# A two-block transformer step on one core: memory values computed in the expert loop, gate and up as two products, norms applied after the products

## The reference, cut to what matters

```python
def first_block(...):
    ...
        h = h + mixed @ w_out[l]
        h = h + hier_moe(rms_norm(h, norm2_gain[l]), w_group[l], b_group[l], w_expert[l],
                         b_expert[l], w_gate[l], w_up[l], w_down[l])
    return rms_norm(h, final_gain)

# one expert: w_gate, w_up 1024 x 512, w_down 512 x 1024
        h = jax.nn.silu(xb @ w_gate[e]) * (xb @ w_up[e])
        return h @ w_down[e]

def second_block(...):
        h = rms_norm_2(x, g_pre_mix[l])
        proj = h @ w_in[l]
        ...
        mem_n = rms_norm_2(mem, g_mem[l])
        c = cross_attention(h, mem_n, w_cq[l], w_ckv[l], w_co[l])

def cross_attention(h, mem_n, w_cq, w_ckv, w_co):
    kv = mem_n @ w_ckv
    k = split_heads(kv[..., :D_MODEL], CROSS_HEADS)
    v = split_heads(kv[..., D_MODEL:], CROSS_HEADS)
```

## Time and profile before

| | us |
|---|---|
| median of three runs | 1629.61 (1627.13 to 1630.34) |
| the profiled execution | 1629.03 |
| its span in the trace | 1627.2 |
| the loop's first expert product | 200.1 |
| last expert's down product | 1120.7 |
| first `in2` product | 1158.9 |

### The profile page before, as it was taken

The page is one execution under the profiler, slowest core; times in us unless marked ns, Lnnn a source line. Parts: engine busy times, 40 slices in busy tenths (PEclk is TensorE's granted clock), DMA queues, the critical chain, the costliest instruction groups (busy, mean ns, idle before and its releaser), DMA issues.

```text
span 1627.2 us, 21987 instructions
## 1 busy us (share of the span) xinstructions
PE 1215.0 (75%) x9589; PEld 752.2 (46%) x9589; DVE 318.9 (20%) x677; ACT 251.4 (15%) x582; POOL 49.3 (3%) x82
## 2 busy tenths in 40 slices
PE   7999956655655665565665565567999899999997
PEld 4566733323432332333332333333445385888843
DVE  1532312211211211221221121122024213100001
ACT  3321311111110110111111111011021212100000
POOL 4101000000000000000000000001000000000000
PEclk9999988978888987997997898898999999999999
DMA  9314499999999999999999999999633251444320
GB/s 351 142 53 163 155 404 430 426 430 427 430 427 430 427 430 427 431 427 431 427 431 427 431 427 431 427 430 403 246 106 104 75 173 51 159 150 147 134 81 28
DMA packets 83105, 493.15 MB, mean 303 GB/s; under 512 B 4768, under 2 KB 28528, under 8 KB 58496
## 3 DMA queue, kind: packets, MB, share of 16 engines
q1 hardware_dynamic: 81088, 486.69, 73.3%
q0 software_dynamic: 1600, 5.17, 1.0%
q10 hardware_dynamic: 384, 0.82, 0.1%
HBM read 491.61 MB, written 1.05 MB: 303 GB/s over the span
## 4 chain that ended last, share of the span: by engine, by line
PE 47%; DMA 46%; DVE 3%; issue 1%; ACT 1%; POOL 1%; SPq 1%; POOLq 0%; DVEq 0%; ACTq 0%
DMA ring<-in_w_up_dram 45%; PE bank L909 10%; PE bank L1141 9%; PE bank L548 6%; PE bank L999 5%; PE bank L1172 5%; PE bank L627 3%; PE bank L568 1%; PE bank L647 1%; DMA ring<-in_w_in_dram 1%; PE bank L536 1%; SPq L381 1%; POOL stat L472 1%; PE bank L764 0%; PE bank L744 0%
## 5 line engine op out<-in xcount | busy, mean ns | idle before, releaser
L909 PE MATMUL bank<-ring,big 128*32 128x256 f32 x4096 | 305.7, 464 | 252.1 <-DMA ring<-in_w_up_dram 234.8
L909 PEld LDWEIGHTS bank<-ring,big 128*32 128x32 f32 x4096 | 174.1, 133 | 378.9 <-issue 342.4
L923 PE MATMUL bank<-ring,big 128*32 128x256 f32 x2048 | 123.8, 382 | 75.5 <-DVE big L1795 62.1
L1141 PE MATMUL bank<-xT,ring 128*128 128x256 f32 (+1 forms) x832 | 153.3, 347 | 0.8 <-issue 0.8
L1141 PEld LDWEIGHTS bank<-xT,ring 128*128 128x128 f32 x832 | 138.0, 191 | 16.5 <-issue 1.6
L1790 DVE TENSOR_TENSOR big<-big,bank 128x128 f32<-128x128 f32 x64 | 23.7, 371 | 525.3 <-ACT big L1355 525.3
L923 PEld LDWEIGHTS bank<-ring,big 128*32 128x32 f32 x2048 | 63.4, 109 | 135.9 <-DVE big L1795 78.9
L1355 ACT ACTIVATE big<-bank 128x128 f32<-128x128 f32 x64 | 17.8, 278 | 511.8 <-PE bank L909 511.8
L548 PE MATMUL bank<-ring,xT 128*128 128x512 f32 x192 | 86.7, 610 | 3.0 <-DVE xT L1478 3.0
L999 PE MATMUL bank<-ring,xT 128*128 128x512 f32 x192 | 86.2, 602 | 0.6 <-ACT xT L1208 0.6
L1799 DVE COPY big<-bank 32x256 f32<-32x256 f32 x128 | 54.3, 424 | 134.7 <-PE bank L923 133.9
(11 more groups left out here) (268 smaller groups left out, 871.0 us busy)
## 6 DMA issues: line engine op xcount, KB each, us to landing
ring<-in_w_gate_dram SPq DMA_DIRECT2D x64, 2048.0 KB, 18.3
ring<-in_w_up_dram SPq DMA_DIRECT2D x64, 2048.0 KB, 22.7
ring<-in_w_down_dram SPq DMA_DIRECT2D x64, 2048.0 KB, 25.1
ring<-in_w_gate_up_dram SPq DMA_DIRECT2D x22, 1024.0 KB, 7.2
ring<-in_w_in_dram SPq DMA_DIRECT2D x14, 1024.0 KB, 12.1
ring<-in_w_down_dram SPq DMA_DIRECT2D x8, 1024.0 KB, 6.5
ring<-in_w_in_dram SPq DMA_DIRECT2D x3, 2048.0 KB, 22.9
ring<-in_w_ckv_dram SPq DMA_DIRECT2D x2, 2048.0 KB, 12.9
```

The lines of the kernel that those rows point to most:

```text
L909: i = pe.matmul(bank[q % 2][TOK * j:TOK * (j + 1), 0:SEQ], xg[:, k, TOK * q:TOK * (q + 1)], w[:, :, k, j * P:(j + 1) * P], start=(k == 0), ...
L923: i = pe.matmul(bank[6 + q % 2][TOK * m:TOK * (m + 1), 0:SEQ], hT[:, q % 2, TOK * k:TOK * (k + 1)], w[:, k, SEQ * m:SEQ * (m + 1)], start= ...
L1141: i = pe.matmul(bank[j % 4][:, gu * SEQ + lo:gu * SEQ + hi], w[:, k, gu, (j % 2) * P:(j % 2 + 1) * P], xT[:, k, lo:hi], start=(k == 0), st ...
```

## The change

- **Memory values in the loop.** The value half of `w_ckv_2` (4 MiB) is no longer part of the weights after the loop. SP loads it before the loop, half into `aux` behind the second expert unit, the rest into `xT` and `mix` once the router has read them. In each pass, between gate and up of q = 3, PE computes 64 of its 1024 columns for both tiles (`memory_values`, 16 products of 64 columns); ACT copies them out, and POOL moves the result to `c_v` after the loop.
- **Gate and up** are two products of 128 columns (32 products each); gate goes to banks 0 and 1, up to bank 5, and each slot is freed by its own product (`moe_g`, `moe_gu`).
- **The pass.** The gather no longer waits for `sel_gate`; its transposes come behind the gather. Combining goes tile by tile.
- **Deferred norms.** After the loop PE transposes the raw `x` tile by tile, the gains of both norms are one product in `col_gain`, and the two rstd factors (`in2_scale`) are applied when `in2` is evacuated. The constants of the second block (`c2`) are loaded from `moe_x` on, as the memory rows stand there until then.
- **Before the loop.** The router works on tables of 8 experts per token, the number of rounds is found before the gates, the mix of tile 0 is finished earlier, and filler steps are moved: 10 and 10 around the transposes of the mix (8 and 8 before), 8 ahead of the loop (12 before). The first gain and three POOL loads move at the start.
- **After the loop** the next norm's transposes stand behind the third product step of the last product (`third`), the out transposes of tile 0 no longer wait for the silu of tile 1, and one evacuation and one maximum are exchanged.

```diff
-                sp.wait_ge(*at("moe_d" if part == "down" else "moe_gu", n))
+                sp.wait_ge(*at({"gate": "moe_g", "up": "moe_gu", "down": "moe_d"}[part], n))
...
+                rows = chunks(t_in["w_ckv_2"][0])[:, :, D:2 * D]
+                if u == 1:
+                    sp.dma_start(aux[:, 0:4 * D].rearrange("p (k c) -> p k c", k=4), rows[:, 0:4, :]).then_inc(S("cvw_in"), 16)
+                if u == 4:
+                    sp.wait_ge(*at("route_mm", TT))
+                    sp.wait_ge(*at("n2_n", TT))
+                    sp.dma_start(xT_[:, :].rearrange("p (k c) -> p k c", k=2), rows[:, 4:6, :]).then_inc(S("cvw_in"), 16)
+                    sp.dma_start(mix_[:, :].rearrange("p (k c) -> p k c", k=2), rows[:, 6:8, :]).then_inc(S("cvw_in"), 16)
...
+            pool.wait_ge(*at("moe_x", 1))
+            load(c2[:, 0:consts["c2"].shape[1]], consts["c2"], "c2_in")
             load(row_gain[:, 0, :], t_in["g_post_mix_2"][0:1, :].to_broadcast([P, D]), "postmix_in")
             for t in range(TT):
                 rstd_tile("pm", t, 38)
+                pool.wait_ge(*at("pm_rstd", t + 1))
+                pool.tensor_tensor(in2_scale[:, t:t + 1], stat[:, 38 + t:39 + t], stat[:, 6 + t:7 + t], ALU.mult
+                                   ).then_inc(S("in2_scale"), 1)
+            for t in range(TT):
+                pool.tensor_copy(c_v[:, t, :], moe_v[t]).then_inc(S("cv_ev"), 1)
...
-            keys(8)
-            wait_T("mix", 0)
+            transposes("mix", mix, 0, 2)
+            keys(10)
             pe.wait_ge(*at("mix_n", 2))
             transposes("mix", mix, 1, 4)
-            keys(8)
+            keys(10)
+            wait_T("mix", 0)
...
-            keys(12)
-            pe.wait_ge(*at("ck_ev", 4))
+            keys(8)
...
-                def hidden_pair(q):
-
-                    arrive("gate", q)
-                    arrive("up", q)
...
+                def hidden(part, q, dst, signal):
+
+                    arrive(part, q)
+                    w = slot(PRE_UNITS + MOE_UNITS.index((part, q))).rearrange("p (k c) -> p k c", k=KD)
                     for k in range(KD):
                         for j in range(4):
-                            i = pe.matmul(bank[q % 2][TOK * j:TOK * (j + 1), 0:SEQ], xg[:, k, TOK * q:TOK * (q + 1)],
-                                          w[:, :, k, j * P:(j + 1) * P], start=(k == 0), stop=(k == KD - 1),
+                            i = pe.matmul(dst[TOK * j:TOK * (j + 1), 0:P], xg[:, k, TOK * q:TOK * (q + 1)],
+                                          w[:, k, j * P:(j + 1) * P], start=(k == 0), stop=(k == KD - 1),
                                           tile_position=(0, TOK * j))
-                    i.then_inc(S("moe_gu"), 1)
+                    i.then_inc(S(signal), 1)
+
+                def memory_values():
+
+                    pe.wait_ge(*at("cvw_in", 48))
+                    pe.wait_ge(*at("moe_v_ev", it + 1))
+                    for t in range(TT):
+                        for k in range(KD):
+                            i = pe.matmul(bank[4][:, t * CV_COLS:(t + 1) * CV_COLS], memT[:, k, t * P:(t + 1) * P],
+                                          cv_weights[k][:, bass.ds(b * CV_COLS, CV_COLS)], start=(k == 0), stop=(k == KD - 1))
+                    i.then_inc(S("moe_v"), 1)
...
                         i.then_inc(S("moe_xg_mm"), 1)
+                pe.wait_ge(*at("moe_selg", it + 1))
+                for t in range(TT):
+                    i = pe.transpose(bank[5][:, t * P:(t + 1) * P], sel_gate[:, t, :], ident)
+                i.then_inc(S("moe_selT_tp"), 1)
                 pe.wait_ge(*at("moe_xg_a", it + 1))
                 pe.wait_ge(*at("moe_xg_v", it + 1))
+                pe.wait_ge(*at("moe_selT", it + 1))
                 for q in range(BATCH):
-                    hidden_pair(q)
+                    hidden("gate", q, bank[q % 2], "moe_g")
+                    if q == BATCH - 1:
+                        memory_values()
+                    hidden("up", q, bank[5], "moe_gu")
                     down(q)
 
...
+                for n in range(4):
+                    t, half = n // 2, n % 2
+                    if n >= 2:
...
-            pe.wait_ge(*at("moe_x", 1))
-            for u in range(2):
-                post_linear("cv", "mm", memT, u, u)
-
-            for t in range(TT):
-                transposes("pm", xn, t)
-            emptied("cv", 2)
+            for t in range(TT):
+                pe.wait_ge(S("moe_xadd"), rounds * (4 * NB) + 1 + 2 * t)
+                transposes("pm", x, t, 4 + 2 * t)
...
-                    act.wait_ge(*at("moe_gu", it * BATCH + q + 1))
+                    act.wait_ge(*at("moe_g", it * BATCH + q + 1))
                     A(eg[:, q % 2, :], bank[q % 2][:, 0:P], ACT.Silu).then_inc(S("moe_e"), 1)
+                    if q == BATCH - 1:
+                        act.wait_ge(*at("moe_v", it + 1))
+                        for t in range(TT):
+                            i = A(moe_v[t][:, bass.ds(b * CV_COLS, CV_COLS)], bank[4][:, t * CV_COLS:(t + 1) * CV_COLS], ACT.Copy)
+                        i.then_inc(S("moe_v_ev"), 1)
...
-            squares("fin", x, 6, mix, lambda t: act.wait_ge(*at("moe_x", 1)))
+            for t in range(TT):
+                act.wait_ge(S("moe_xadd"), rounds * (4 * NB) + 1 + 2 * t)
+                square("fin", x, 6, mix, t)
+                evac_T("pm", 1, tiles=(t,))
...
             def in2_evac(u):
                 act.wait_ge(*at("in2_mm", 2 * u + 1))
-                A(proj2[:, 0, IN2_UNITS[u]:IN2_UNITS[u] + 512], bank[0][:, :], ACT.Copy).then_inc(S("in2_ev0"), 1)
+                if u == 0:
+                    act.wait_ge(*at("in2_scale", 1))
+                if u == 4:
+                    act.wait_ge(*at("cv_ev", TT))
+                A(proj2[:, 0, IN2_UNITS[u]:IN2_UNITS[u] + 512], bank[0][:, :], ACT.Copy, scale=in2_scale[:, 0:1]).then_inc(S("in2_ev0"), 1)
...
+            gate(0)
+            evac_T("mix2", tiles=(0,))
+            gate(1)
+            evac_T("mix2", tiles=(1,))
...
+            of_group = rg[2].unsqueeze(3).to_broadcast([P, TT, NG, EPG])
...
+            link(V.tensor_reduce(r8[0], rt[0].rearrange("p t (g e) -> p t e g", g=NG), AX.X, ALU.add))
+            first_max(r8[1], r8[0], EPG, rank8, rs[1], r8[2])
...
+                        dve.wait_ge(*at("moe_gu", it * BATCH + q + 1))
                         V.tensor_tensor(hx[:, q % 2, :, :].rearrange("p j f -> p f j"),
                                         eg[:, q % 2, :].rearrange("p (f j) -> p f j", j=4),
-                                        bank[q % 2][:, P:2 * P].rearrange("p (f j) -> p f j", j=4),
+                                        bank[5][:, 0:P].rearrange("p (f j) -> p f j", j=4),
                                         ALU.mult).then_inc(S("moe_h"), 1)
...
-            scaled("pm", x, 38)
-            evac_odd("cv", 2, lambda u: c_v[:, 1, 512 * u:512 * (u + 1)], lambda u: bank[(2 * u + 1) % 4][:, :])
             evac_T("pm", 1)
+            scaled("fin", x, 6, row_gain[:, 1, :], x, "x_final")
...
+            moba_max(0)
             in2_evac(2)
-            moba_max(0)
```

More of the change, by code:

```diff
@@ L565, in linear_T @@
                 for jj in range(2):
+                    if jj == 1 and middle:
+                        middle()
                     for m in range(2):
@@ L929, in _ @@
                 pe.wait_ge(*at("moe_sel", it + 1))
[L930 to L933 removed]
+                pe.wait_ge(*at("moe_xadd", it * 4 + 3))
                 for k in range(KD):
```

223 lines of the change are left out of this document (113 added, 110 removed), and 2 rows, old and new, of the table mask.

## The result

The changed kernel takes **1573.91 us** (median of 4 runs, 1572.94 to 1574.97), the kernel before 1628.37 beside it (1623.28 to 1630.34): a ratio of 0.967, 95% interval 0.9646 to 0.9694. The forecast of 1583.0 had the sign and most of the mechanisms, but was 9.1 us too long: the median lies 1.1 us under its own bounds (1575 to 1592) and 0.1 us under the wider range that takes in the fourth and fifth rivals (1574 to 1597). The profiled execution took 1574.33 us with a span of 1572.5 (before: 1627.2), so 54.7 us have to be found where 46.0 were forecast.

A forecast was written before the change was run, and what follows sets the result against it. The loop was taken as bound by its transfers, its end moving with the first slot release, the rest by PE. 6.3 + 1 + 28.9 + 9.8 = 46.0 off 1629.0 gave 1583.0 us, own bounds 1575 to 1592, wider range 1574 to 1597.

The forecast's parts named there:

- fourth rival: Behind the loop: the factors or `c2` come late and hold `in2`'s banks, costing 8 to 10 us: 1592; chance 0.10.
- fifth rival: Values' weights collide with the stream, or values run cold ahead of up at loop's end: 9.8 or 4.5 us; chance 0.08.
- What bounds the kernel: Transfers set the loop's length, 58.8 us a pass; its end moves only with the first release of a slot.
- step 6: After `in2`: waits before `out2`, the next norm's transposes and the first exponentials shrink; 9.8 us gained, bounds 5 and 11.
- Step 1: From the start to the first release of a slot: 6.3 us gained, bounds 3 and 9.
- The mixed heads: Ahead of the loop: removing PE's wait of 2.42 us and the lower-clock work behind it gains 4.0 us.
- third rival: In the loop every record has a fixed price of about 62 ns; pass 60.3 us, kernel 1607 us; chance 0.05.
- Step 2: The value weights' 4 MiB transfer, queued ahead of the loop, costs nothing; 5 us if half delayed the first passes.
- Step 3: PE's work in a pass, 47.5 us at 37 ns a record, stays hidden under 58.8 us of transfers; nothing added.
- second rival: PE becomes the loop's bound, from 59.0 ns a record, and the kernel slower; 1722 us at 76 ns; chance 0.05.
- Step 4: At the loop's end, up to the last down product: 1 us gained, bounds 2.3 and -3.5.
- Step 5: From the last down product to `in2`: 9.3 us in place of 38.2, 28.9 us gained.

The follow-up runs named there:

- the experiment brings back the wait of 2.42: Changed kernel with the order around the mixed heads as before the change (8 fillers behind each transpose, 12 ahead of the loop): 1577.16 us.
- the doubled pairs: Changed kernel with gate and up as pairs of 256 columns again, slots released after the pair, each pair run twice: 1626.24 us.
- The experiment brings back 3.8 of the 5.1: Changed kernel with both gates ahead of both tiles' evacuations before `out2`, on ACT and DVE, as before the change: 1577.78 us.
- the yardstick: The changed kernel itself, unaltered, run beside its variants on the same chip: 1574.28 us, 0.967 of the kernel before.

## Why the prediction was right, and where it was not

**What bounds the kernel.** Right. Four kernels with a first reload at 191.91, 192.72, 193.59 and 197.96 have their last gate product 905.5 to 905.7 us later. Each of the four stretches gained at least what was forecast, so the sum is not right by luck; inside step 6 a term 1.1 too large stands against one 2.9 too small.

**Step 1, 6.3 forecast, 12.0 came,** outside its bounds of 3 and 9. This is the term that was mis-sized most.
- "At the start of the kernel ... nothing" is the sentence that failed: 2.2 us. The memory rows do come from POOL, but POOL asks for them only when the first weights have landed, and that is 15.12, not 17.38, as three small loads no longer stand in front. The time that I took as unchanged hangs on a wait that the change moves. The run with the loads put back shows that their place alone moves it, by 3.2 us.
- The mixed heads gave 4.2 (out products at 137.93 instead of 142.54, less the 2.2, and with four fillers, 1.8 us, more ahead of them). The forecast was 4.0; the experiment brings back the wait of 2.42 and leaves open why the clock fell before: there it fell behind this wait, in the experiment behind the same 2.42 us it did not.
- The router gave 0.9 for 0.7; no run takes it alone.
- From the place products to the first gate product 3.0 us were gained beside the four fillers, for 0.3. The loop entry that was to "stay" at 1.99 did not: `sel` is ready earlier and PE waits only 0.93. And the gather took 3.83 us where it took 5.25. The wait behind the gather gave the 0.4 that remain (0.71 for 1.12).
- From the start of the first product to the first reload it is 2.15 us in place of 3.86, 1.7 for 1.3. The price was 28.9 ns (3.70 us for 128 records), the end of the bounds that stands for columns alone, and not 37. The third rival falls with it.

**Step 2, nothing.** Nearly right: from the first reload to the last down product it is no longer than before (915.6 and 916.7). But the weights of that product landed 915.6 us after the first reload, and by the forecast's estimate (1118.35) some 914.4 before: the stream may have become 1.2 us longer, and no run shows by what.

**Step 3, hidden.** Right for the changed kernel: passes of 58.7 us, a gate product of 1.95, values 3.7 us for 3.8. But the reasoning was weaker than it sounded. "Even at 57.2 ns 57.9, all below 58.8" fails in the doubled pairs, which keep PE about as long (7.11 us for 128 records): 61.4 us a pass. The second rival therefore seems to begin before its 59 ns, though in those pairs gate's slot is also held longer. And a whole rival was missing, the size of the loop's code: the change took it from 426 to 714 records a pass, and 128 more would have eaten 46.6 of the 54.7 us. That it stopped short of that was not foreseen by me; it was luck.

**Step 4, 1 us.** 1.1 came. The down product's wait of 1.15 us ends with its weights; the hand-over alone takes 0.84 where the weights are there, so they hold it up by 0.3. The last gate ran slow, the values behind it did not (3.7 us from 1100.8 to 1104.53), and the fifth rival falls for this kernel.

**Step 5, 28.9.** 29.2 came, with the factors in time: the first evacuation of `in2` started at 1123.79 with both factors ready by 1122.7, and `in2` ran without a gap. The fourth rival falls. The experiment with the norms ahead of the projection shows the two parts of this term.

**Step 6, 9.8.** 12.4 came, outside its bounds of 5 and 11. `out2` gave 5.1 of its 6.2 (2.97 + 10.16 before, 0.89 + 7.10 after): a wait of 0.89 stayed. The experiment brings back 3.8 of the 5.1. Both norm waits are gone (2.9). The term that was too small is the exchange before the first exponentials: 0.7 forecast, 3.6 came. Not a part of the wait of 1.84 went but all of it, the transposes behind it took 0.66 us for 1.06, and the ten `in2` records behind these took 4.46 us and not 5.79:

```profile
1162.99 0.66 PE L1074 MATMUL bank<-c,ring 128*128 128x128 f32 x4
1163.48 4.46 PE L1033 MATMUL bank<-ring,xT 128*128 128x512 f32 x10
```

That the exchange did it is argued from its place; no run takes it back, nor the two norm waits. The remaining 0.8 are small.

## What to carry to other kernels

When a loop is bound by its transfers, work from behind it can go into it free of charge, but ask what that work was hiding: here 7.9 of the 29.2 us gained behind the loop came only with the norms, which had to be taken out of the way as well. "Hidden because PE's sum is below the transfers' sum" needs a margin (the doubled pairs, 57.9 against 58.8 by the sum, took 61.4), and the count of PE's instructions in the loop belongs in the sum: look at the instruction queue's packets. And a time that is called unchanged should be followed back to what it waits for.

## What the runs showed of the chip

- fp32 records of 128 columns with 32 stationary columns, four side by side, took 28.9 ns each, those of 64 columns 16.6 ns. The Trainium skill, "TensorE: Matmul & The Clock Gate", section "Back-to-back issue gap", has a floor near 25 ns for up to 64 columns, and about 62 ns for each matmul with hardware decode off. The 16.6 lie under the first and both under the second; here four records run side by side, in four column strips, which that table does not treat.
- PE's code was read once (27 packets) with 714 weight loads and 714 matmuls a pass, and, by the 16 packets that come with each 256 instructions more, again in every pass with 842 of each (163 packets), at a price of 46.6 us in 16 passes; the largest stop stands at the loop's top, 5.7 us in the pass shown.
- With three small loads (a mask and two gains) put ahead in POOL's queue, the rate from 12 to 16 us was 214 GB/s and not 329, while the DMA engines were busy 0.99 and not 0.92.
- The last pass of the loop ran at a granted clock of 0.54 in the one profiled execution with gate's early release taken back, and there down began 4.0 us later behind gate than in the yardstick.
